# Scores ahead of transpositions in the 64-step loop of a hybrid attention stack, with head, tail and inverses rearranged

## The reference, cut to what matters

```
h = h + rms_norm(mixer(rms_norm(h, g0)), g1)
h = h + rms_norm(conv_ffn(rms_norm(h, g2)), g3)
```

```
s = q @ k.T * scale - slope * distance        (causal)
p = exp(s - max) / max(sum, 1e-30)
out += gate * (p @ v)
```

## Time and profile before

| | us |
|---|---|
| median of 3 runs (2573.37 to 2575.04) | 2573.88 |
| the profiled execution | 2574.38 |
| its span | 2572.6 |

### The profile page before, as it was taken

One profiled execution on the slowest core, in us unless ns is written; L12 is line 12 of the kernel. 1 busy time (PEld: TensorE's weight loads), 2 busy tenths in 40 slices (PEclk: granted clock), 3 DMA queues, 4 the chain that ended last, 5 costly groups with the idle time before them and its releaser, 6 DMA issues.

```text
span 2572.6 us, 38307 instructions
## 1 busy us (share of the span) xinstructions
PE 2514.6 (98%) x13336; PEld 2072.8 (81%) x13336; DVE 1607.4 (62%) x2773; ACT 1184.5 (46%) x2035; POOL 467.3 (18%) x514
## 2 busy tenths in 40 slices
PE   8999999999999999999999999999999999999997
PEld 6987778888788678888878878888779778788886
DVE  7598577664353847667256677664386884766733
ACT  4467554443232845444245554443254684544431
POOL 2035321110010612111010021110010552111100
PEclk9999999999999999999999999999999999999999
DMA  4410123333233023332321123333233002233331
GB/s 160 142 34 2 42 83 98 98 98 98 87 99 99 9 66 99 98 97 90 103 85 57 42 82 99 98 98 98 79 116 122 18 2 58 87 94 97 90 106 49
DMA packets 61909, 210.91 MB, mean 82 GB/s; under 512 B 8528, under 2 KB 10320, under 8 KB 61776
## 3 DMA queue, kind: packets, MB, share of 16 engines
q1 hardware_dynamic: 61776, 209.13, 26.3%
HBM read 207.01 MB, written 2.10 MB: 81 GB/s over the span
## 4 chain that ended last, share of the span: by engine, by line
PE 91%; DVE 5%; ACT 1%; issue 1%; POOL 1%; DMA 0%; DVEq 0%; SPq 0%; POOLq 0%; ACTq 0%
PE psum L305 21%; PE psum L306 21%; PE psum L307 21%; PE psum L1310 3%; PE psum L1331 3%; PE psum L928 2%; PE psum L930 2%; PE psum L929 2%; PE psum L333 2%; PE psum L335 2%; PE psum L339 2%; PE psum L1297 1%; PE psum L1296 1%; PE psum L1093 1%; DVE h L501 1%
## 5 line engine op out<-in xcount | busy, mean ns | idle before, releaser
L305 PE MATMUL psum<-xh,w_hi 128*128 128x512 f32 x1712 | 666.6, 389 | 0.0
L306 PE MATMUL psum<-xh,w_lo 128*128 128x512 f32 x1712 | 666.1, 389 | 0.0
L307 PE MATMUL psum<-xl,w_hi 128*128 128x512 f32 x1712 | 666.1, 389 | 0.0
L267 DVE TENSOR_TENSOR w_lo<-w_raw,w_hi 128x1024 fp32r<-128x1024 f32 x226 | 284.1, 1269 | 527.5 <-ACT w_hi L261 525.7
L261 ACT ACTIVATE w_hi<-w_raw 128x1024 fp32r<-128x1024 f32 x226 | 236.2, 1057 | 590.6 <-PE psum L307 464.8
L307 PEld LDWEIGHTS psum<-xl,w_hi 128*128 128x128 f32 x1712 | 321.3, 188 | 66.8
L305 PEld LDWEIGHTS psum<-xh,w_hi 128*128 128x128 f32 x1712 | 321.4, 188 | 66.6 <-issue 0.2
L306 PEld LDWEIGHTS psum<-xh,w_lo 128*128 128x128 f32 x1712 | 321.4, 188 | 66.4
L709 DVE TENSOR_TENSOR w_lo<-w_raw,w_hi 128x1024 fp32r<-128x1024 f32 x160 | 209.3, 1308 | 253.6 <-ACT w_hi L705 253.6
L680 POOL TENSOR_TENSOR cv<-cv 128x512 f32<-128x512 f32 x88 | 133.9, 1521 | 793.7 <-ACT cv L634 773.0
L705 ACT ACTIVATE w_hi<-w_raw 128x1024 fp32r<-128x1024 f32 x160 | 168.4, 1052 | 234.8 <-PE psum L307 234.7
(11 more groups left out here) (221 smaller groups left out, 4027.1 us busy)
## 6 DMA issues: line engine op xcount, KB each, us to landing
w_raw<-w_up SPq DMA_DIRECT2D x176, 512.0 KB, 3.6
w_raw<-w_down SPq DMA_DIRECT2D x88, 512.0 KB, 3.6
w_raw<-nsa_in SPq DMA_DIRECT2D x56, 512.0 KB, 4.3
w_raw<-sb_in SPq DMA_DIRECT2D x24, 512.0 KB, 3.7
w_raw<-nsa_out SPq DMA_DIRECT2D x16, 512.0 KB, 3.6
w_raw<-swa_in SPq DMA_DIRECT2D x10, 512.0 KB, 3.8
w_raw<-sb_out SPq DMA_DIRECT2D x8, 512.0 KB, 3.6
w_raw<-swa_out SPq DMA_DIRECT2D x8, 512.0 KB, 3.6
```

The source lines that it names most:

```text
L267: nc.vector.tensor_tensor(w_lo[:, u % RING, :], w_raw[:, u % RING, :], w_hi[:, u % RING, :].bitcast(F32), ALU.subtract).then_inc(split_don ...
L305: nc.tensor.matmul(bank(p, o), wh[:, k, o, :], xhi(k), start=(first and k == 0), stop=False)
L306: nc.tensor.matmul(bank(p, o), wl[:, k, o, :], xhi(k), start=False, stop=False)
L307: mm = nc.tensor.matmul(bank(p, o), wh[:, k, o, :], xlo(k), start=False, stop=(last and k == 1))
```

## The change

Five edits, none of which alters the arithmetic of a value.

1. In the 64-step loop TensorE takes scores(t+4), transposes(t), values(t-1).
2. VectorE's loop order becomes copy(t), biased(t+4), floor(t+3), inverse(t+3), then window keys or queries as before. Ahead of the loop, floor and inverse of step 1 come after `window_keys`, and those of step 2 after biased(3).
3. SP's head: chunk pair 0 of x, norm gains, weight unit 0, identity, then the rest.
4. ScalarE's head: xh of both chunks of a pair, the pair's w_hi, then the two squares.
5. Tail: VectorE keeps chunks 4, 5, 6, 7, 3. Chunks 0, 1, 2 go to GpSimd: ScalarE multiplies their u by the gain before the last squares, GpSimd multiplies by rn and adds to h. SP sends 4, 0, 5, 6, 1, 7, 3, 2.

```diff
+        LAST_V, LAST_G = (4, 5, 6, 7, 3), (0, 1, 2)
+        def act_last(act, s, u, g_post):
+            act.wait_ge(u_done, 4 * (s + 1))
+            for c in LAST_G:
+                nc.scalar.activation(u[:, c, :], u[:, c, :], ACT.Copy, scale=norm_g[:, g_post, c:c + 1]).then_inc(ug_done, 1)
+        def pool_last(pool, s, u):
+            pool.wait_ge(r_done, 2 * s + 2)
+            for k, c in enumerate(LAST_G):
+                pool.wait_ge(ug_done, k + 1)
+                nc.gpsimd.tensor_tensor(u[:, c, :], u[:, c, :], rn[:], ALU.mult).then_inc(ur_done, 1)
+                pool.wait_ge(ur_done, k + 1)
+                nc.gpsimd.tensor_tensor(h[:, c, :], h[:, c, :], u[:, c, :], ALU.add).then_inc(hp_done, 1)
...
                     high(c)
-                    square(c, c)
                     if c % 2:
                         split_hi(act, c // 2)
+                        square(c - 1, c - 1)
+                        square(c, c)
...
             for t in range(STEPS):
-                transposes(t)
                 if t + 4 < STEPS:
                     scores(t + 4)
+                transposes(t)
                 if t:
                     values(t - 1)
...
-            for t in range(2):
-                floor(t)
-                inverse(t)
+            floor(0)
+            inverse(0)
             window_keys()
+            floor(1)
+            inverse(1)
             biased(2)
             biased(3)
+            floor(2)
+            inverse(2)
             for t in range(STEPS):
                 it, x = t // 16, t % 16
-                i = step_of(t)[3]
-                if i == 0:
+                if step_of(t)[3] != 1:
                     copy(t)
-                if t + 2 < STEPS:
-                    floor(t + 2)
-                if i >= 2:
-                    copy(t)
-                if t + 2 < STEPS:
-                    inverse(t + 2)
                 if t + 4 < STEPS:
                     biased(t + 4)
+                if t + 3 < STEPS:
+                    floor(t + 3)
+                    inverse(t + 3)
...
-            sp.dma_start(norm_g[:], ins["norm_g"]).then_inc(consts_landed, 16)
-            sp.dma_start(ident[:], ins["ident"]).then_inc(consts_landed, 16)
             for k in range(DC // 2):
                 sp.dma_start(h[:, 2 * k:2 * k + 2, :], ins["x"][:, 2 * k:2 * k + 2, :]).then_inc(x_landed[k], 16)
+                if k == 0:
+                    sp.dma_start(norm_g[:], ins["norm_g"]).then_inc(consts_landed, 16)
                 if k < AHEAD:
                     load_unit(sp, ins[kinds[0] + "_in" if kinds[0] else "w_up"][k], k)
+                if k == 0:
+                    sp.dma_start(ident[:], ins["ident"]).then_inc(consts_landed, 16)
```

More of the change, by code:

```diff
@@ L197, in hybrid_layers @@
         h_done = sem("h_done")
+        ug_done = sem("ug_done")
+        ur_done = sem("ur_done")
+        hp_done = sem("hp_done")
         hs_done = sem("hs_done")
@@ L504, in dve_update @@
                 dve.wait_ge(r_done, 2 * s + 2)
-                for c in range(DC):
-                    if c >= 2:
-                        dve.wait_ge(h_done, 8 * s + c - 1)
+                for c in LAST_V:
                     update(c)
-                dve.wait_ge(h_done, 8 * s + DC)
+                dve.wait_ge(h_done, 8 * s + len(LAST_V))
                 dve.sem_inc(evac_v, 1)
@@ L699, in act_ffn @@
             split_his(act, d0 + FC // 2 + 2, FC // 2 - 2)
+            if l == len(kinds) - 1:
+                act_last(act, s, ffn_u, 4 * l + 3)
             act_squares(act, s, 1, plan.down_p[l] + 1, d0 + FC)
@@ L2276, in _ @@
             last = per * len(kinds) - 1
-            for c in range(DC):
-                sp.wait_ge(h_done, 8 * last + c + 1)
+            for c in (4, 0, 5, 6, 1, 7, 3, 2):
+                if c in LAST_V:
+                    sp.wait_ge(h_done, 8 * last + LAST_V.index(c) + 1)
+                else:
+                    sp.wait_ge(hp_done, LAST_G.index(c) + 1)
                 sp.dma_start(out[:, c, :], h[:, c, :]).then_inc(out_landed, 16)
@@ L2343, in _ @@
                 pool_sum_squares(pool, ch, s)
-                if not last:
+                if last:
+                    pool_last(pool, s, ffn_u)
+                else:
                     pool_h_squares(pool, s)
```

## The result

The changed kernel takes 2594.53 us (median of 4 runs, 2594.1 to 2596.98) against 2574.14 for the kernel before on the same chip (2573.37 to 2575.04): ratio 1.0081, 95% interval 1.0069 to 1.0094. It is slower by 20.4 us, and the forecast was 23.9 slower. In the profiled executions the span went from 2572.6 to 2592.6, so 20.1 us are to be found in the traces. Scores are now L1315 and L1316, transposes L1329, values L1350, exps L1395, ScalarE's copy L1403 and its output copy L1414, act_query L1376, dve_query L1382, biased L1449, VectorE's copy L1459, floor L1480, inverse L1485, weighted L1529.

A forecast was written before the change was run, and what follows sets the result against it. TensorE, busy for 98% of the span, was taken to pace the kernel. Terms of 6.0 + 17.1 - 2.1 + 1.0 + 0.4 + 3.4 - 1.9 + 0 gave +23.9, thus 2597.8 us against the median; 8-in-10 range 2576 to 2608.

The forecast's parts named there:

- switches: TensorE's changes between kinds of work in both loops: +0.05 us a step from the new order, +6.0 us.
- queries: At group ends in both loops, TensorE waits for VectorE's late query, 1.2 us at x = 10, 1.65 at x = 14: +17.1 us.
- step 12 for GpSimd: In the loops, inverse right behind biased removes two waits of transposes for GpSimd at step 12: -2.1 us.
- window keys: In the first 16 steps, scores(8) wait for VectorE's first window key, 0.5 us in each loop: +1.0 us.
- entry: At loop entry, the PSUM bank comes 0.15 us earlier, but scores(4) wait about 0.35 for biased(2): +0.4 us for both loops.
- clock: Idle times added in the loops cause two drops of TensorE's granted clock: +3.4 us.
- tail: At the kernel's end, GpSimd finishes last, chunk 2 ready 9.3 us after rn: -1.9 us.
- head: At the start, x is issued earlier but both engines still wait for the identity; TensorE starts as before: 0 us.
- Only the switches: Rival in the loops: queries come in time, so query and clock terms drop out; 2577.3 us, chance 0.23.
- Faster: Rival in the loops: switches are free, GpSimd wait and tail gains remain; 2567 to 2570 us, chance 0.08.
- VectorE as the pace: Rival in the loops: floor's in-line wait delays every step, 0.35 us a round of four; 2608 us, chance 0.12.
- The tail's six at 2.10: Rival in the tail: GpSimd's six operations at 2.10 us end later than VectorE's sixteen did; +3.5 us, within the remaining 0.05.

The follow-up runs named there:

- experiment 2: The kernel before with only TensorE's order changed to scores, transposes, values; VectorE's order, head and tail as before: 2580.4 us, ratio 1.0019.
- experiment 10: The kernel before with the new tail alone (VectorE keeps five chunks, GpSimd and ScalarE take three): 2572.23 us, ratio 0.9989.
- experiment 3: The changed kernel with VectorE's low part of the next group's query moved ahead of floor(t+3) and inverse(t+3): 2579.14 us, ratio 1.0015.
- experiment 1: The changed kernel with TensorE's order put back to transposes, scores, values; VectorE's new order, head and tail stay: 2581.3 us, ratio 1.0025.
- experiment 5: The changed kernel with TensorE's transposes put back ahead of scores and VectorE's query put ahead of floor and inverse: 2575.72 us, ratio 1.0007.
- experiment 9: Against a kernel with old loop orders, new entry, tail and head (identity on its own semaphore): floor and inverse of step 12 one step earlier; 2567.17 us.
- old_head: The changed kernel with the head of before, both SP's and ScalarE's head edits undone: 2595.56 us, ratio 1.0082.
- ident_apart: The changed kernel with the identity on a semaphore of its own, for which only TensorE waits: 2593.72 us, ratio 1.0076.
- out_late: The changed kernel with ScalarE's output copy moved from x = 13 to x = 14 of a group: 2588.95 us, ratio 1.0059.

## Why the prediction was right, step by step

| term | forecast | measured | from |
|---|---|---|---|
| switches | +6.0 | +7.2; alone +6.1 | PE busy in the windows (1.1 of it belongs to the waits, see below); experiment 2 |
| queries | +17.1 | +16.1 | the row of twelve waits |
| step 12 for GpSimd | -2.1 | -2.1 in waits | the row is gone |
| window keys | +1.0 | +1.6 | two waits, 0.96 and 0.61 |
| entry | +0.4 | -1.4 | 11.37 to 10.67, and 12.98 less a drop of 1.6 to 10.68 |
| clock | +3.4 | about +0.3 | -1.6 in the second loop; +0.8 on the way to the first loop, +0.5 and +0.6 outside |
| tail | -1.9 | -1.9 | 15.02 to 13.15; experiment 10 |
| head | 0 | 0 | PE starts at 10.42 where it was 10.43 |
| sum | +23.9 | +19.8 | against 20.1 in the spans |

**The queries** decided the case, and the chain was right in its links: 3.94 us at x = 14 against 3.85 reckoned, and twelve waits at the two places. The sizes: at x = 14 they are 1.51 (1.65 forecast), at x = 10 they are 1.03 (1.2), except 1.44 in the first group. The chain was not the part that was mis-sized but PE's own work beside it, 2.44 (3.94 less the wait of 1.50) where 2.2 was reckoned. Experiments 3 and 4 each take one link out, and its part of the wait goes.

**The switches.** 0.05 a step was forecast; 0.051 is measured where PE's order is the only thing changed, 0.060 in the full change. The difference of 0.55 us a loop is no switch either. The order of PE is the same in both kernels, but the change has seven more waits of scores in a loop, and behind each the scores start 0.07 later than the idle time says. At 234.06 the eight value products ahead of them start at 231.90; where nothing waits they take 0.59, so the scores are 1.57 late and PE is idle for 1.50. The missing 0.07 is counted as busy, because the last product before a wait is shown to its modelled end, and 7 x 0.07 is 0.49 of the 0.55. So of the measured 7.2 some 1.1 belongs to the waits, and both terms were nearer than the table says: switches 6.1, queries 16.9.

Where the 0.05 arises is not where the prediction saw it. It took the 0.34 of the first fp32r product behind values for a price of the 64-column tile. But that product takes 0.32 behind transposes too, so the tile can be 0.02 of it. In the rows of i = 3 the scores became 0.08 shorter (1.11 to 1.03) and the transposes 0.11 longer (0.85 to 0.96); the two stand-ins of the prediction had the sum right (2.00 against 1.99), and why transposes cost more between scores and values is open. That the order of the three kinds would be free, as the prediction drew it from the weight load's rule (the Trainium skill, TensorE: Matmul & The Clock Gate, Step-by-step: what each phase is for), isn't borne out: 3.04 us a loop in experiment 2. The 0.34 against 0.23, which the prediction held against it, doesn't show that.

**Where the prediction was off.** Two terms failed, the entry and the clock, and a third was put down to the wrong edit (step 12, below). At the entry, "the bank comes 0.15 earlier, of 1.6" was mis-sized: with floor(1) moved, scores(2) wait 0.34 instead of 1.6 in each loop, so floor had held window_keys by its own wait for the exponentials, not by its length. It is there in the trace of the kernel before, 0.83 long:

```profile
155.22 0.22 DVE L1461 TENSOR_SCALAR rsums<-rsums 128x2 f32<-128x2 f32 x1 [0.83 <-ACT scores L1376]
```

The inverse and the window keys follow, these at 155.55. In the changed kernel the window keys start 0.08 behind the inverse of step 0 (155.05 and 155.13). I had priced an instruction by its duration where it was its wait that counted, the very effect that I had reckoned at the queries. The new wait for biased(2), 0.33, came as forecast (0.35). And the clock: none of twelve idle times of 1.0 to 1.5 us in the two loops of the changed kernel was followed by a drop, and the one of before in the second loop went too. The trace has four drops, all outside the loops, where the trace of before has two outside and one inside (tail not counted). The errors partly cancelled: 1.8 too much at the entry, 3.1 at the clock and 1.0 at the queries, 1.2 too little at the switches and 0.6 at the window keys. Two bounds of the prediction don't follow from their own numbers: twelve waits of 0.3 are 3.6, not 2, and six operations of GpSimd at 2.10 with 0.11 between them take 13.2, which is 2.0 more than the 11.2 of before and not 1.6. Neither touches the sum.

**The step-12 term** agrees in the row, but not for the reason under which it stood, edit 2 alone. Edit 1 alone takes these two waits from 2.1 to 0.4 (experiment 2), because the transposes come later. Edit 2 without edit 1 leaves 1.0 with the query late (experiment 1) and 2.6 with the query early (experiment 5). And experiment 9 shows that such a wait's length overstates what it is worth: 1.92 of waits gone, 0.76 of loop gained.

**The tail.** Right in size, partly by luck. Forecast was GpSimd as the last, 9.3 after rn, with 0.8 of interference, and the last transfer behind it as before. GpSimd ends at 2588.97 and VectorE's chunk 3 at 2589.51, 8.65 after VectorE's first, which is 0.65 sooner. But from there to the end it takes 3.1 where it took 2.4 (2570.15 to 2572.6). SP sends in a fixed order, 3 before 2, so chunk 2, ready at 2588.97, waits behind chunk 3 and is issued last, at 2589.92. With 2 sent before 3, the last issue would be that of 3, at 2589.55, some 0.4 sooner; that is an estimate from these issues, and no run here has it. The contention is with VectorE's operations that have both operands in SBUF, and both sides pay: VectorE's pair 3.04 instead of 1.44, GpSimd's last 1.59 instead of 1.26. With the Trainium skill (GPSIMD Engine Reference, Key points: contention with VectorE's instructions of two SBUF inputs) the trace agrees: the operations with a PSUM operand kept 0.75 and 0.69.

**The head.** The row shows what was forecast: x earlier, the wait for the identity longer, PE where it was. Of the identity, the transfers' landings (the first line is the weight unit, issued at 1.68, the second the identity, issued at 2.14) show that it came in at 6.6, just behind the unit at 6.5 (issue to landing, each for its one transfer):

```profile
DMA to landing us min/median/max: 4.8/4.8/4.8
```

```profile
DMA to landing us min/median/max: 4.5/4.5/4.5
```

The Trainium skill (DMA: Bandwidth & Descriptors, Queues, rings and completion order) allows it to come in first; here it didn't.

**The rivals.** Only the switches: refuted by the row of twelve waits; its condition, queries in time, is experiment 3, 2579.1 against the 2577.3 that it gave. Faster: refuted; its switches are not free, and the chain of 3.94 was longer than PE's 2.44 us. VectorE as the pace: not the 2608 that it gave, but there is something in it, since VectorE's new order costs 2.8 us a loop with transposes first even where no query is late (experiment 5). With scores first it has little of that: in query_early no weight load of a transpose waits for copy, and its loop is only 1.6 longer than that of s_first_only. The tail's six at 2.10: refuted.

## What to carry to other kernels

An in-line wait on a helper engine delays everything behind it, so price an instruction that you move by the time at which its input is there, and look what is queued behind it. Two reorderings, each nearly covered by the slack of the other's old order, can cost far more together (11.6 us a loop) than apart (2.6 and 5.5): test them one at a time, and keep those that pay (here the tail and the entry, 2567.9 us). A wait that is gone from the list of waits is not time gained until the window around it is shorter. And read the waits of the weight loads beside those of the matmuls: 22 waits for copy in experiment 5 stood in the one list and only two in the other.

## What was new of the hardware

- **PE's first rise moves.** In twelve traces the distance between the first products falls from 0.43 to 0.23 us at 3.0 to 6.2 us after PE's first product. The granted clock reads 1.00 on both sides of it (kernel before and changed kernel); that it is the clock is inferred from the distance, since four such products inside the last line's stretch, at a granted 0.50, take 0.43 each (2218.51 to 2220.21). Each us of delay lengthens the way from there to the first loop by about 0.5 (140.14 at 3.0, 141.07 at 5.05, 141.59 at 6.2). That is more than any edit of the head was worth.
- **The same idle time doesn't always cost the clock.** In the kernel before, in tail_alone and in s_first_only, an idle time of 1.6 at the entry is followed by 3.4 us at a granted clock of 0.5 in the second loop, and in the first loop by none. Of the twelve waits of 1.0 to 1.5 in each of four kernels (changed, old_head, ident_apart, out_late) one alone was followed by a drop, in ident_apart at 2058.2. A drop inside the loop costs 1.6 (ident_apart's second loop is 154.15 long, its first 152.55), one in the products outside about 0.5 (from the first loop to the second 1709.4 to 1709.6 us with none, 1710.0 to 1710.1 with one, 1710.5 to 1710.6 with two, 1711.1 with three). Here is one of 3.4 us behind the second loop of the changed kernel.

```profile
2217.10:2220.50 3.40, 3.40 (x13) 3.01 (x13) 3.33 (x6) 2.83 (x5) 0.00 (x0) 0.50 0.00 0
```
